# Two more weight slots in the rope tables' space around the first out-projection, and longer fillers in the four-step attention blocks

## The chip, the cores and the metric

One Trainium2 chip, 8 cores, one program on all of them. Each core computes 2 of the 16 sequences and exchanges nothing with the others. The metric is the device time of the slowest core in microseconds.

## The reference

One decoder layer on x of (16, 2048, 1024): a feed-forward half-step, a token mixer, a second feed-forward half-step, a last RMSNorm. Every sub-layer has an RMSNorm, a shift and scale on its input and a gate on its output, all three from `c @ w_ada`.

```python
u = modulate(rmsnorm(h, ffn1_norm), sh1, sc1)
h = h + 0.5 * g1 * ((silu(u @ w_gate) * (u @ w_up)) @ w_down)      # 1024 -> 2816 -> 1024
u = modulate(rmsnorm(h, mix_norm), sh2, sc2)
proj = u @ w_in                                                     # q, k, v and latents
# group A: 4 heads of differential attention, two softmax maps of width 64 each, rope on q and k
# group B: 4 heads of latent attention, width 64 + 32 (rope on the 32), causal as well
h = h + g2 * (concat([od, om]) @ w_out)
u = modulate(rmsnorm(h, ffn2_norm), sh3, sc3)
h = h + 0.5 * g3 * ((silu(u @ w_gate2) * (u @ w_up2)) @ w_down2)
return rmsnorm(h, final_norm)
```

## The kernel before, in words

**Tiles.** A core holds two sequences s = 0, 1 of 2048 positions, each as four tiles tt of 512 positions, with the 1024 channels as 8 pieces of 128 partitions. Intermediate h lives in DRAM. A tile is 2 MB in f32.

**Two lanes.** The program is written out in full by Python generators; each `yield` gives a cost. Lane F (`lane_f`, `ffn_group` L580) is the feed-forward work; lane M (`lane_m`, `mixer` L967) is the token mixer. The loop at the end of `build` takes one step of lane M, adds what it yields to `credit`, and then takes steps of lane F until their costs (0.216, named MM, for one matmul of 512 columns) have used the credit up. So each yield of lane M is the amount of filler, in these credit us, that is put behind that step on PE. Where lane M yields None it stands, and lane F goes on alone. When lane M is done, lane F runs alone. The order on each engine is the order in which the generators issue; engines then run by semaphores.

**Lane F.** First sequence 0, then sequence 1 while mixer(0) runs (tiles named 10 to 13 in the code), then the second feed-forward of sequence 0 (20 to 23) while mixer(1) runs, then, once mixer(1) is done, that of sequence 1 in two groups of two tiles. For one tile, `unit` L596 runs 11 times: two units of 2048 columns of weights (gate and up), 4 x 8 matmuls, tanh on ACT and two products on DVE. Then 8 down steps of 22 matmuls on two weight units of 1408 columns, with a residual piece that is loaded (`Residual`) and stored. In the two-tile groups the first tile's two first units come before the second tile's.

**Weights.** `Ring` L189 holds the slots: NWF = 6 for lane F (wf), 4 for the mixer (wm). `plan` lists all loads in order; `pump` issues the next one as soon as a slot is free; `release` frees a slot at the end of its use and pumps. A pair of wf slots is a unit or a down step, so with 6 slots the pairs of the next two are on their way. The loads of wf go through the SP queue, in order with all its other transfers; a transfer that waits for an engine holds up those behind it. The wm loads are casts on the POOL queue.

**The norms of lane F** are side generators (`norm_gen` L465): load a tile into XT, some steps of lag (8, or 14 where `dense`), 8 squares and 8 statistics matmuls, one step for the rsqrt on ACT, 8 applies. `f_step` advances them by one step for each step of lane F, or for every second one while both lanes run. With `dense` it is every one. A group that needs a tile waits in program order until its norm is written out.

**mixer(s).** At its start it loads the first two tiles (MIXP, and MUS with a row of 2 KB pieces) and the rope tables (`load_tab` L767, eight transfers of 128 KB into TAB). Norms of four tiles, each step yielding W_NORM. For a = 0, 1: projections of two heads with rope (it reads TAB), then `attention` L790 over two heads (g = 0, 1), each with four blocks qc = 0 to 3 of 4 qc + 4 steps. Then load_tab again with the latent layout, latents, and for a = 0, 1 up-projections (`rope` again) and `attention` with one group for two latent heads. Then the out-projection: for each tile 8 output pieces m, with a store of h and a load of the next tile's residual in halves, through the SP queue. TAB is idle from the last up-projection of mixer(0) to the start of mixer(1).

**attention.** Step i issues the scores of step i+1, exp on ACT, and the value matmuls of step i. At a block's end the sums are copied to `accsb` and `evac` puts the rest on `evq`: for a differential head ten small DVE parts ("D") and a transpose on PE ("T"). These run in the next block's steps; in a block of four steps all ten D parts are issued in its first step, and T at the earliest two steps later. At the start of each attention call `evq` is empty. A step yields at L864:

```python
yield W_ATT * (1.0 if r == 0 else 0.6)      # W_ATT = 1.2; r = 0 where the step has all four query blocks
```

In a block with qc = 0 the four steps have r = 0, 1, 2, 3. A step with a T yields 0.5 and 0.6 of W_ATT instead.

Of the kernel before, what the change touches and what calls it, by code (L numbers as in the profile page):

```python
# [157 lines left out]
NWF = 6  # L158
NWM = 4
MM = 0.216  # L160
W_ATT = 1.2
# [27 lines left out]
class Ring:  # L189


    def __init__(self, n):
        self.free = list(range(n))
        self.pending = collections.deque()
        self.loaded = {}
        self.on = False

    def plan(self, key, load):
        self.pending.append((key, load))
# [10 lines left out]
        return self.loaded[key]  # L210

    def release(self, key):
        self.free.append(self.loaded.pop(key))
        self.pump()

def build():
# [28 lines left out]
    sgu = [dscr(f"sgu{i}", [22, 128, 2048], BF16) for i in range(2)]  # L245
    sdn = [dscr(f"sdn{i}", [16, 128, 1408], BF16) for i in range(2)]

    with contextlib.ExitStack() as es:
# [4 lines left out]
        def sb(name, shape, dt):  # L253
            return es.enter_context(nc.sbuf_tensor(name, list(shape), dt))
# [24 lines left out]
        WFR = [Res(f"wf{i}") for i in range(NWF)]  # L279
        WM = [sb(f"wm{i}", [128, 2048], BF16) for i in range(NWM)]  # L280
        WMR = [Res(f"wm{i}") for i in range(NWM)]
        XT = sb("xt", [128, 4096], F32)
        xtR = [Res(f"xt{k}") for k in range(NK)]
        HST = [tile(f"hst{i}", [128, 512], F32) for i in range(3)]
# [65 lines left out]
        def dma_group(into, of, stream, parts):  # L350

            first = S.dma("sp", r=of, w=into, stream=stream, out=parts[0][0], in_=parts[0][1])
            rest = [S.dma("sp", stream=stream, out=o, in_=i) for o, i in parts[1:]]
            for o in rest:
                o.deps = list(first.deps)
                first.dval = o.dval
            for o in rest:
                o.dval = first.dval
# [37 lines left out]
        def wf_plan(fi, ps, first, units):  # L396
            for kind, j in units:
                n = 2048 if kind == "gu" else 1408
                if first:
                    wf.plan((fi, ps, kind, j), cast_load(WF, WFR, "wf", (wgu if kind == "gu" else wdn)[fi][j], n))  # L400
                else:
                    def load(b, kind=kind, j=j, n=n):
                        res = (sguR if kind == "gu" else sdnR)[fi][j]
                        assert res.w is not None
                        S.dma("sp", r=[res], w=[WFR[b]], stream=f"wf{b}", out=WF[b][:, 0:n], in_=(sgu if kind == "gu" else sdn)[fi][j])
                    wf.plan((fi, ps, kind, j), load)

        GU = [("gu", j) for j in range(22)]
# [358 lines left out]
        def load_tab(s, diff):  # L767
            if diff:
                parts = [(slice(32 * r, 32 * r + 32), si, 64 * (1 - si), 32) for r in range(4) for si in range(2)]
            else:  # L770
                parts = [(slice(64 + 16 * r, 80 + 16 * r), si, 32 + 64 * (1 - si), 16) for r in range(2) for si in range(2)]
            dma_group(tabR, tabDR[s], "tab", [(TAB[rows, si * 2048:(si + 1) * 2048].rearrange("p (t n) -> p t n", t=4),
                                               tabD[s, :, d0:d0 + n, :].rearrange("t p n -> p t n")) for rows, si, d0, n in parts])

        evq = collections.deque()
# [14 lines left out]
        def attention(groups, scale, evac, extra=()):  # L790
# [47 lines left out]
            for i in range(n):  # L838
                g, qc, j, r, last = steps[i]
                left = 4 * qc + 4 - j  # L840
                if evq and evq[0][0] == "T" and i >= tmin[0]:
                    tick(1)
                    pv(i)
                    yield 0.5 * W_ATT
                    if i + 1 < n:
                        qk(i + 1)
                    yield 0.6 * W_ATT
                else:
                    nd = 0
                    for kind, fn in evq:  # L850
                        if kind == "T":
                            break
                        nd += 1
                    if i + 1 < n:
                        qk(i + 1)
                    pv(i)
                    if not last:
                        for _ in range(-(-nd // max(1, left - 3))):
                            if evq and evq[0][0] == "D":
                                tick(1)  # L860
                                tmin[0] = i + 2
                    if extra and left > 2 and psF.free:
                        extra.popleft()()
                    yield W_ATT * (1.0 if r == 0 else 0.6)  # L864
            while extra:
                extra.popleft()()
            att[0] = False
# [99 lines left out]
        def mixer(s):  # L967
# [15 lines left out]
            def mstep(n):  # L983
# [7 lines left out]
                        mside.popleft()  # L991
                return False

            load_tab(s, True)
            for a in range(2):
                for tt in range(4):
# [105 lines left out]
            for a in range(2):  # L1102
# [34 lines left out]
                if a == 1:  # L1137
                    wm.release((s, "uq"))
                    wm.release((s, "ukv"))
                extra = []  # L1140
                if s == 0 and a == 0:
                    extra = [lambda: None] * 10 + [functools.partial(ada_unit, j, wm, WM, WMR) for j in range(32, 36)]
# [38 lines left out]
            for tt in range(4):  # L1181
                srcs = [gran(MIXB, mixR, h * 4 + tt) for h in range(4)] + [om_slot(h, tt) for h in range(4)]
                nxt = om_norm(tt + 1) if tt < 3 else iter(())
                for m in range(NK):
                    b = wm.get((s, "wo", m // 2))
                    wv = WM[b][:].rearrange("p (k n) -> p k n", k=8)
# [305 lines left out]
```

How the kernel before makes its waits and increments, by code:

```python
            def run(ename, eng):  # L109
                seen = {}
                for o in self.ops[ename]:
                    need = {}
                    for p in o.deps:
                        if p.dma:
                            key, val, sem = ("d", p.dsem), p.dval, dsem[p.dsem]
                        else:
                            key, val, sem = ("e", p.eng), p.tick, esem[p.eng]
                        if seen.get(key, 0) < val and need.get(key, (0, None))[0] < val:
                            need[key] = (val, sem)
                    waits = list(need.items())
                    fold = None
                    if FOLD_WAITS and waits and not o.dma:
                        fold = waits.pop()
                    for key, (val, sem) in waits:
                        eng.wait_ge(sem, val)
                        seen[key] = val
                    ins = getattr(eng, o.fn[0])(**o.fn[1])
                    if fold is not None:
                        key, (val, sem) = fold
                        ins._wait_ge(sem, val)
                        seen[key] = val
                    if o.dma:
                        ins.then_inc(dsem[o.dsem], 16)
                    elif o.inc:
                        ins.then_inc(esem[ename], 1)
                if ename == "sp":
                    for p in final_waits:
                        eng.wait_ge(dsem[p.dsem], p.dval)
```

## Time and profile before

| | us |
|---|---|
| median of 3 runs | 3069.78 |
| lowest, highest | 3059.08, 3070.62 |
| the profiled execution's own time | 3066.18 |
| its span, slowest core (core 1) | 3064.6 |
| the other cores' spans | 3034.3 to 3063.4 |
| PE busy | 2842.9 |
| DVE, ACT busy | 1403.2, 1254.9 |
| mean granted TensorE clock of core 1 | 0.980 |

The span goes from the first to the last instruction of the slowest core. All durations below come from this one execution. "PE" is the matmuls, "SPq" the instructions of the SP queue that issue transfers; x is a count. An idle time in brackets stands before the row's first instruction, with the operation that released it. Every operation is recorded at line 127, the helper that issues it, so groups are told apart by their tiles: `uf,wf` are gate/up matmuls, `actf,wf` down-projection, `mu,wm` and `mixb,wm` the mixer's, `pt,ones_sb` and `btf,ones_sb` the statistics of the mixer's and of lane F's norms, `cm_sb,obf` the transposes of evicted outputs.

### The profile page before, as it was taken

To read this page: it belongs to the slowest core of one execution; us is meant where nothing else is said; L and a number is where in the kernel's file an instruction comes from. 1 tells how busy PE (TensorE), PEld (TensorE's weight loads), DVE (VectorE), ACT (ScalarE), POOL (GpSimd) and SP (SyncE) were. 2 spreads that over 40 slices of the span, in tenths; PEclk is the share of its full clock that TensorE was granted. 3 is DMA by queue.
4 is the path that set the end of the run, shared out by engine and by line. 5 is a ranking of instruction groups with operands and counts; after the bars stand their busy time and mean duration, and the time that the engine had idled before them with its cause. 6 is when DMAs were issued, how large, how long until landed. Compare 5 with 4: busy or idle time off the path is not lost.

```text
span 3064.6 us, 42690 instructions; the slowest of 8 cores (3034.3 to 3064.6 us)
## 1 busy us (share of the span) xinstructions
PE 2842.9 (93%) x16528; PEld 1356.0 (44%) x16528; DVE 1403.2 (46%) x2808; ACT 1254.9 (41%) x1750; POOL 75.0 (2%) x147
## 2 busy tenths in 40 slices
PE   3799998999899999999978999999999999999998
PEld 1344443444454444544434445444454444444443
DVE  3564215344455455244446545654535443532532
ACT  2421205345434456444245443555755524322311
POOL 1000000000000000000000000000000000000000
PEclk9899999999999999999989999999999999999999
DMA  9886685475914934553883333434345278336436
GB/s 193 170 160 154 168 218 158 134 206 129 219 62 115 201 99 105 119 153 112 247 265 117 96 110 113 140 100 131 86 137 162 99 251 262 138 106 203 165 119 224
DMA packets 144138, 470.76 MB, mean 154 GB/s; under 512 B 17376, under 2 KB 21216, under 8 KB 129760
## 3 DMA queue, kind: packets, MB, share of 16 engines
q1 hardware_dynamic: 127600, 399.80, 40.9%
q0 software_dynamic: 16336, 68.23, 14.2%
q8 instruction: 131, 2.15, 0.3%
q14 instruction: 71, 0.58, 0.1%
HBM read 452.83 MB, written 100.66 MB: 181 GB/s over the span
## 4 chain that ended last, share of the span: by engine, by line
PE 76%; DMA 11%; ACT 5%; DVE 5%; issue 1%; SPq 1%; POOL 0%; ACTq 0%; DVEq 0%; POOLq 0%
PE psall L127 76%; ACT pt L127 3%; DMA wf<-sdn 2%; DMA wm<-w_ada 1%; DMA h<-hst 1%; DMA h<-qk 1%; DMA wf<-w_ada 1%; DMA accsb<-pos 1%; DMA hst<-xL 1%; SPq L127 1%; ACT mu L127 1%; DVE mu L127 1%; DVE ftm L127 1%; DVE accsb L127 1%; ACT L127 1%
## 5 line engine op out<-in xcount | busy, mean ns | idle before, releaser
L127 PE MATMUL psall<-uf,wf 128*128 128x512 bf16 x4224 | 1037.1, 384 | 30.5 <-DVE hst L127 6.6
L127 ACT ACTIVATE pt<-psall 128x1024 bf16<-128x1024 f32 (+3 forms) x520 | 453.0, 872 | 457.3 <-PE psall L127 455.8
L127 PEld LDWEIGHTS psall<-uf,wf 128*128 128x128 bf16 x4224 | 400.2, 99 | 462.5 <-issue 28.7
L127 PE MATMUL psall<-actf,wf 128*128 128x512 bf16 x2112 | 516.3, 386 | 16.8 <-DMA wf<-sdn 16.8
L127 ACT ACTIVATE ftf<-psall 128x512 f32<-128x512 f32 x352 | 210.1, 597 | 660.0 <-PE psall L127 645.9
L127 DVE SCALAR_TENSOR_TENSOR ftf<-ftf,psall 128x512 f32<-128x512 f32 x352 | 241.1, 685 | 448.0 <-ACT ftf L127 416.8
L127 PE MATMUL psall<-mu,wm 128*128 128x512 bf16 (+2 forms) x1312 | 328.6, 381 | 12.5 <-ACT mu L127 8.2
L127 PE MATMUL psall<-mixb,wf 128*128 128x512 bf16 x1408 | 321.4, 383 | 8.6 <-ACT mixb L127 4.9
L127 PEld LDWEIGHTS psall<-actf,wf 128*128 128x128 bf16 x2112 | 200.7, 99 | 227.6 <-issue 20.2
L127 DVE SCALAR_TENSOR_TENSOR hst<-psall,SC,hst 128x512 f32<-128x512 f32 x120 | 90.0, 750 | 426.1 <-PE psall L127 315.3
L127 DVE TENSOR_TENSOR actf<-ftf,psall 128x512 bf16<-128x512 f32 x264 | 180.9, 685 | 195.2 <-PE psall L127 192.7
L127 PE MATMUL psall<-va,pt 128*128 128x129 bf16 x3264 | 268.5, 222 | 1.7 <-ACT pt L127 1.6
L127 PE MATMUL psall<-qk 64*128 64x512 bf16 (+1 forms) x960 | 201.3, 354 | 44.6 <-ACT pt L127 36.9
L127 PEld LDWEIGHTS psall<-va,pt 128*128 128x128 bf16 x3264 | 202.0, 98 | 65.8 <-issue 39.8
L127 PEld LDWEIGHTS psall<-mixb,wf 128*128 128x128 bf16 x1408 | 137.3, 98 | 178.4 <-ACT mixb L127 8.1
L127 PEld LDWEIGHTS psall<-mu,wm 128*128 128x128 bf16 (+2 forms) x1312 | 130.2, 102 | 177.5 <-ACT mu L127 16.6
L127 DVE TENSOR_TENSOR ftm<-tab,psall 128x512 f32<-128x512 bf16 (+1 forms) x208 | 139.6, 683 | 114.6 <-PE psall L127 94.5
L127 ACT ACT_TABLE_LOAD x92 | 118.0, 1283 | 158.5 <-PE psall L127 156.4
L127 PEld LDWEIGHTS psall<-qk 64*128 64x128 bf16 (+1 forms) x960 | 55.5, 94 | 228.4 <-ACT pt L127 143.0
L127 ACT ACTIVATE btf<-xt 128x512 bf16<-128x512 f32 x164 | 97.9, 623 | 99.1 <-DMA xt<-xL 43.0
L127 ACT ACTIVATE btm<-psall 128x512 bf16<-128x512 f32 (+1 forms) x104 | 61.7, 594 | 136.1 <-PE psall L127 135.3
L127 DVE COPY accsb<-psall 128x387 f32<-128x387 f32 x144 | 74.0, 514 | 57.6 <-PE psall L127 55.3
(113 smaller groups left out, 1991.5 us busy)
## 6 DMA issues: line engine op xcount, KB each, us to landing
wf<-sgu SPq DMA_DIRECT2D x242, 512.0 KB, 3.9
wf<-sdn SPq DMA_DIRECT2D x192, 352.0 KB, 4.1
h<-hst SPq DMA_DIRECT2D x120, 256.0 KB, 4.5
xt<-h SPq DMA_DIRECT2D x30, 1024.0 KB, 7.1
wm<-w_ada POOLq DMA_DIRECT2D x32, 512.0 KB, 12.1
hst<-xL SPq DMA_DIRECT2D x64, 256.0 KB, 6.4
qk<-h SPq DMA_DIRECT2D x16, 1024.0 KB, 6.5
h<-qk SPq DMA_DIRECT2D x16, 1024.0 KB, 9.7
```

The source lines that it names most:

```text
L127: ins = getattr(eng, o.fn[0])(**o.fn[1])
```

## The change

`Ring` learns to lend: `lend` adds slots to the free ones, `ask_back` takes those out that are free and keeps the others from coming back, `returned` says whether none is still loaded. Two slots, number 6 and 7, are the two halves of TAB (512 KB each). They are lent in mixer(0) after the last up-projection, asked back at the start of its fourth out-projection tile, and each mixer waits (`yield None`) until they are returned before it loads its tables. Loads into them also wait for the readers of TAB, and table loads for the readers of the slots. The yield of an attention step with qc = 0 becomes 1.2 where it has no eviction part and 1.7 x 1.2 = 2.04 where it has.

```diff
--- before.py
+++ after.py
@@ -194,6 +194,21 @@
         self.pending = collections.deque()
         self.loaded = {}
         self.on = False
+        self.lent = []
+        self.back = True
+
+    def lend(self, slots):
+
+        self.lent, self.back = list(slots), False
+        self.free += self.lent
+        self.pump()
+
+    def ask_back(self):
+        self.back = True
+        self.free = [b for b in self.free if b not in self.lent]
+
+    def returned(self):
+        return not any(b in self.lent for b in self.loaded.values())
 
     def plan(self, key, load):
         self.pending.append((key, load))
@@ -210,7 +225,9 @@
         return self.loaded[key]
 
     def release(self, key):
-        self.free.append(self.loaded.pop(key))
+        b = self.loaded.pop(key)
+        if not (self.back and b in self.lent):
+            self.free.append(b)
         self.pump()
 
 def build():
@@ -279,6 +296,9 @@
         WFR = [Res(f"wf{i}") for i in range(NWF)]
         WM = [sb(f"wm{i}", [128, 2048], BF16) for i in range(NWM)]
         WMR = [Res(f"wm{i}") for i in range(NWM)]
+        WF += [TAB[:, 0:2048], TAB[:, 2048:4096]]
+        WFR += [Res("wf6"), Res("wf7")]
+        lentR = {NWF: tabR[0:4], NWF + 1: tabR[4:8]}
         XT = sb("xt", [128, 4096], F32)
         xtR = [Res(f"xt{k}") for k in range(NK)]
         HST = [tile(f"hst{i}", [128, 512], F32) for i in range(3)]
@@ -402,7 +422,7 @@
                     def load(b, kind=kind, j=j, n=n):
                         res = (sguR if kind == "gu" else sdnR)[fi][j]
                         assert res.w is not None
-                        S.dma("sp", r=[res], w=[WFR[b]], stream=f"wf{b}", out=WF[b][:, 0:n], in_=(sgu if kind == "gu" else sdn)[fi][j])
+                        S.dma("sp", r=[res], w=[WFR[b]] + lentR.get(b, []), stream=f"wf{b}", out=WF[b][:, 0:n], in_=(sgu if kind == "gu" else sdn)[fi][j])
                     wf.plan((fi, ps, kind, j), load)
 
         GU = [("gu", j) for j in range(22)]
@@ -769,7 +789,7 @@
                 parts = [(slice(32 * r, 32 * r + 32), si, 64 * (1 - si), 32) for r in range(4) for si in range(2)]
             else:
                 parts = [(slice(64 + 16 * r, 80 + 16 * r), si, 32 + 64 * (1 - si), 16) for r in range(2) for si in range(2)]
-            dma_group(tabR, tabDR[s], "tab", [(TAB[rows, si * 2048:(si + 1) * 2048].rearrange("p (t n) -> p t n", t=4),
+            dma_group(tabR + WFR[NWF:], tabDR[s], "tab", [(TAB[rows, si * 2048:(si + 1) * 2048].rearrange("p (t n) -> p t n", t=4),
                                                tabD[s, :, d0:d0 + n, :].rearrange("t p n -> p t n")) for rows, si, d0, n in parts])
 
         evq = collections.deque()
@@ -861,7 +881,7 @@
                                 tmin[0] = i + 2
                     if extra and left > 2 and psF.free:
                         extra.popleft()()
-                    yield W_ATT * (1.0 if r == 0 else 0.6)
+                    yield W_ATT * ((1.7 if nd else 1.0) if qc == 0 else 1.0 if r == 0 else 0.6)
             while extra:
                 extra.popleft()()
             att[0] = False
@@ -991,6 +1011,8 @@
                         mside.popleft()
                 return False
 
+            while not wf.returned():
+                yield None
             load_tab(s, True)
             for a in range(2):
                 for tt in range(4):
@@ -1137,6 +1159,8 @@
                 if a == 1:
                     wm.release((s, "uq"))
                     wm.release((s, "ukv"))
+                    if s == 0:
+                        wf.lend([NWF, NWF + 1])
                 extra = []
                 if s == 0 and a == 0:
                     extra = [lambda: None] * 10 + [functools.partial(ada_unit, j, wm, WM, WMR) for j in range(32, 36)]
@@ -1181,6 +1205,8 @@
             for tt in range(4):
                 srcs = [gran(MIXB, mixR, h * 4 + tt) for h in range(4)] + [om_slot(h, tt) for h in range(4)]
                 nxt = om_norm(tt + 1) if tt < 3 else iter(())
+                if s == 0 and tt == 3:
+                    wf.ask_back()
                 for m in range(NK):
                     b = wm.get((s, "wo", m // 2))
                     wv = WM[b][:].rearrange("p (k n) -> p k n", k=8)
```

## Rows read from the trace of the kernel before

**Rows 1.** The page, busy time, share of the span and instructions of each engine.

```profile
PE 2842.9 (93%) x16528; PEld 1356.0 (44%) x16528; DVE 1403.2 (46%) x2808; ACT 1254.9 (41%) x1750; POOL 75.0 (2%) x147
```

**Rows 2.** Windows of 40 us: length, busy us of each engine, PEclk, DMA share, GB/s.

```profile
1480.00:1520.00 40.00, 40.00 (x187) 18.09 (x185) 17.43 (x26) 8.36 (x13) 1.09 (x2) 1.00 0.74 218
1520.00:1560.00 40.00, 28.84 (x120) 12.06 (x118) 12.99 (x20) 11.39 (x19) 1.06 (x2) 0.87 1.01 285
1560.00:1600.00 40.00, 28.45 (x108) 11.32 (x109) 15.85 (x26) 15.31 (x24) 0.00 (x0) 0.83 0.80 263
```

**Rows 3.** Waits of PE, 1310 to 1525 us: total us, times, longest; first of four.

```profile
PE psall L127 <- ACT pt L127: 4.9, 10, 1.2
```

**Rows 4.** Timeline of the SP queue at the end of the first out-projection (start, us, what).

```profile
1519.16 9.95 SPq L127 DMA_DIRECT2D h<-qk  x2
1529.27 1.07 SPq L127 DMA_DIRECT2D wf<-sdn  x2
...
1531.83 0.85 SPq L127 DMA_DIRECT2D mixb<-h  x2
1532.72 5.80 SPq L127 DMA_DIRECT2D mu<-h  x2
1538.67 14.46 SPq L127 DMA_DIRECT2D tab<-tabD  x8
1553.28 1.82 SPq L127 DMA_DIRECT2D wf<-sdn  x4
```

**Rows 5.** Timeline of PE in the same stretch, with idle time and releaser in brackets.

```profile
1549.75 0.61 PE L127 MATMUL psall<-pt,ones_sb 128*128 128x512 bf16 x1 [7.44 <-ACT pt L127]
...
1567.18 1.89 PE L127 MATMUL psall<-actf,wf 128*128 128x512 bf16 x4 [9.46 <-DMA wf<-sdn]
...
1579.56 1.97 PE L127 MATMUL psall<-mu,wm 128*128 128x512 bf16 x7
```

**Rows 6.** DMA view of 1525 to 1570 us.

```profile
DMA packets 5030, 12.92 MB, mean 287 GB/s; under 512 B 484, under 2 KB 1508, under 8 KB 4516
```

**Rows 7.** Timeline of PE: the transposes in the four second-head blocks with qc = 0.

```profile
776.44 0.79 PE L127 MATMUL psall<-cm_sb,obf 128*128 128x128 bf16 x4 [2.29 <-DVE obf L127]
...
1023.39 0.79 PE L127 MATMUL psall<-cm_sb,obf 128*128 128x128 bf16 x4 [2.81 <-DVE obf L127]
...
1787.13 0.79 PE L127 MATMUL psall<-cm_sb,obf 128*128 128x128 bf16 x4 [2.81 <-DVE obf L127]
...
2023.53 0.73 PE L127 MATMUL psall<-cm_sb,obf 128*128 128x128 bf16 x4 [1.21 <-DVE obf L127]
```

**Rows 8.** Windows of 10 us around these four transposes.

```profile
770.00:780.00 10.00, 7.51 (x50) 3.62 (x48) 6.65 (x25) 3.40 (x5) 0.00 (x0) 0.84 1.17 145
...
1020.00:1030.00 10.00, 6.63 (x27) 2.36 (x25) 6.10 (x20) 1.96 (x4) 0.49 (x1) 0.66 0.79 99
...
1780.00:1790.00 10.00, 6.99 (x47) 3.23 (x45) 7.81 (x27) 2.65 (x4) 0.00 (x0) 0.86 0.13 37
...
2020.00:2030.00 10.00, 8.20 (x60) 3.65 (x57) 8.33 (x28) 4.59 (x7) 0.00 (x0) 1.00 0.27 90
```

**Rows 9.** Timeline of PE, a first-head block with qc = 0.

```profile
1699.86 0.34 PE L127 MATMUL psall<-qk 64*128 64x384 bf16 x2 [0.25 <-ACT pt L127]
```

**Rows 10.** Timeline of PE behind the second mixer.

```profile
2567.98 4.44 PE L127 MATMUL psall<-actf,wf 128*128 128x512 bf16 x12 [2.38 <-DMA wf<-sdn]
...
2579.38 0.38 PE L127 MATMUL psall<-btf,ones_sb 128*128 128x512 bf16 x1
...
2585.63 13.98 PE L127 MATMUL psall<-uf,wf 128*128 128x512 bf16 x64
2599.45 2.75 PE L127 MATMUL psall<-mixb,wf 128*128 128x512 bf16 x12
```

**Rows 11.** Timeline of ACT in the same stretch.

```profile
2589.91 0.81 ACT L127 ACTIVATE mixb<-xt,SC 128x512 bf16<-128x512 f32 x1
```

**Rows 12.** Window from 2600 us to the last group's end.

```profile
2600.00:3058.00 458.00, 453.90 (x2103) 205.48 (x2100) 170.82 (x251) 115.64 (x180) 0.00 (x0) 1.00 0.48 155
```


## The prediction

> **What bounds the kernel now.** I read the page's busy shares first. TensorE (PE) is busy 93% of the span, VectorE and ScalarE under half [rows 1]. The matmuls are not changed, so only two things can move the time: PE's idle time of about 220 us and stretches at a lower granted clock. So I then looked for the stretches where PE idles near the code that is edited, in the windows, the timeline and the DMA view.
>
> Around the first out-projection the windows say where nothing is lost: in 1480 to 1520 us PE is busy 40.00 of 40 us. The loss comes right behind it: 28.8 and 28.5 of 40 us, at a granted clock of 0.87 and 0.83 [rows 2]. There the SP queue issues, in one burst, the last store of the out-projection, two down-projection weights, two residual tiles, 2 MB for the next mixer's first tile, 2 MB for its second and 1 MB of rope tables. The eight table issues hold the queue for 14.46 us; only behind them come the next four weights, at 1553.28 [rows 4]. PE stops twice: 7.44 us for the first square of the mixer's norm (its tile lands late) and 9.46 us for a down-projection weight [rows 5]. In 45 us the engines moved 12.92 MB, 287 GB/s [rows 6]: this burst is bound by transfers.
>
> **Edit 1: the lent slots.** The feed-forward lane (F) runs 11 gate/up units of 32 matmuls and then 8 down steps of 22 for each tile; the mixer lane (M) hands it credit at each yield, 0.216 a matmul. Walking the code's yields: at the lend point F is in the last down step of tile 2, and the ring holds that step's pair and the pairs of units 0 and 1 of tile 3. The lent pair takes unit 2, then every fourth pair: units 6 and 10. From then on each pair is issued one unit earlier. In the time of the loan the four waits of PE that the view lists are for ScalarE and VectorE, the longest 4.9 us in ten pieces, and none is for a weight [rows 3]; so that alone is worth 0. ask_back comes in the fourth out-projection tile, with F in unit 10, after unit 9's release. So the weights of down steps 0, 1 and 2 are all issued before the burst; today step 2's come behind it. Unit 10's release returns the pair 2.7 credit us before the second mixer starts: the new wait yields nothing, the table load finds its readers done, and nothing queues behind it. Cost of that wait: 0. If the pair were late, M would stand and F would run ahead by the same amount, with the price of edit 2's end.
>
> **Edit 2: the fillers.** In the four-step blocks (qc = 0) a step yields 1.2 instead of 0.72 when it has no eviction, and 2.04 instead of 1.2 when it has. The first block of each of the four attention calls of a mixer gains 3 x 0.48 = 1.44, the same block of a second head 0.84 + 0.48 + 0.48 = 1.80. Two mixers: 2 x (4 x 1.44 + 2 x 1.80) = 18.7 us of F work that is done earlier, 9.36 of it before the first mixer ends.
>
> **What the fillers win.** In the second heads' blocks PE waits for the evicted output to be scaled before it transposes it: 2.29, 2.81, 2.81 and 1.21 us [rows 7]. Of the new filler 0.84 + 0.48 = 1.32 us lie ahead of that transpose: 3 x 1.32 + 1.21 = 5.2 us. The three longer waits stand in windows of 0.84, 0.66 and 0.86 granted clock, the 1.21 one in a window of 1.00 [rows 7, 8]. The missing 1.6 + 3.4 + 1.4 = 6.4 us of clock lie partly over idle time; I take half, 3 us. The other blocks wait some 0.25 us at one step [rows 9]: eight of them, 2 us. Bounds: 5 us (the waits by 1.32, no clock) and 15 (all of it). A loss is excluded: it is work moved, not added. Sum: -10.
>
> **The burst, moved against F.** Today step 2's weights (needed 16.2 credit us after the second mixer starts) are what PE waits for. In the new order the first weights behind the burst are step 3's, needed 889.3 - 877.7 = 11.6 after it. Measured from the last store's issue (1528.8, just before its row ends), today the weight lands at 1567.18, 38.4 us later [rows 4, 5]. The new burst lacks 0.7 MB of weights and 0.5 MB of residual tiles ahead of it; at 287 GB/s [rows 6] that is 4.2 us, so step 3's weights land at 34. PE gets to them after 11.4 + 8 statistics matmuls (0.216 each) = 13.1 us: one wait of 21, in which the norm's tile lands too, against 7.44 + 9.46 today. Behind it lie 13.1 + 1.7 us of work to the first projection and about 2 of slow clock: 51 after the store. Today the projection starts at 1579.56 [rows 5], 50.8 after it. F is 9.4 ahead of M both at the start and at the end of this stretch. So the term is 0: the wait is not removed, it is one step later and one piece. Bounds: 12 us won (the weights land at 22, were the table issues not held up) and 6 lost (they land as late as today, and the clock falls longer).
>
> A page of the Trainium skill speaks for more here. "DMA: Bandwidth & Descriptors", under Bandwidth, gives each core of a pair that streams about 358 GB/s. At that rate the same bytes would land at 34 x 287 / 358 = 27, an estimate, and the sum would be 7 us lower than mine. The trace disagrees over the burst, with its 287 GB/s and 1,508 packets below 2 KB.
>
> **Where the moved work is missed.** At the second mixer's end F is 18.7 further on: 30 instead of 49 credit us of its tile 3 are left. They hide the norms of the next group's two tiles, one side step to each F step; the first takes 29 steps, the second 34. Today the 49 hold some 61 steps, and the second norm is done in time: its statistics end at 2579.76, the first tile's 64 matmuls begin at 2585.63, and only behind them, at 2599.45, is the second tile used [rows 10]. In the new order 30 credit us hold 38 steps and the 64 matmuls 16: 54 for 63, nine short. The last nine (the rsqrt and the eight applies) are then issued with no matmul between. What shows is the chain from the last statistic to the last apply, 2579.76 to 2590.72 today, 11 us [rows 10, 11]. Its last calls also queue behind lane F's; eight applies of 0.81 [rows 11] and some 2 for the rsqrt are 8.5. Less the 1.7 of matmuls that follow the applies one by one, 7. With the clock behind it 8.5: today 12 matmuls behind an idle 2.38 us took 4.44 instead of 2.6 [rows 10]. That wait of 2.38 itself, for weights beside a tile load, I leave as it is. After 2600 PE is busy 453.9 of 458 us [rows 12] and nothing else can be lost or won. Bounds: +3 (the applies run ahead of PE) and +13 (the whole chain and the clock). Sum: +8.5.
>
> **Sum.** -10 + 0 + 8.5 = -1.5 us on the profiled execution's 3066.2. The median of the runs shown is 3.6 above that execution: 3069.8 - 1.5 = 3068.
>
> **Rivals.**
> *The wait behind the burst shrinks.* If the table issues take their 14.46 us [rows 4] only because transfers are queued up in front of them, less in front lets step 3's weights go out up to 12 us earlier. For it: the rate reaches only 287 GB/s while SP stands. Against: POOL's casts of the mixer's weights and 5 MB of tiles and tables are unchanged. The Trainium skill's rate above would give a part of it, 7 us. It gives 3068 - 12 = 3056, and with the fillers' upper bound 3051. Chance 0.22.
> *The fillers fill nothing.* The 1.32 us are spent in other steps than the one that waits, or PE's order makes the wait reappear at the exp of the next step. Then the end's 8.5 stand alone, less 2: 3076. Against: the wait is a chain of some 7 us on VectorE that starts before both filled steps. Chance 0.12.
> *Slower: the wait behind the burst grows.* Place: down step 3 of F's tile 3. The cover is 11.6 against 16.2 today. The new order loses from the point where the weights land more than 34 us after the last store; each us later is a us of PE. If the mixer's tile and the tables go first and the weights land at 46, it costs 12 + 2 of clock: 3082. For it: the same queue, weights last. Chance 0.11.
> *The change doesn't do what it says:* the loan carries three pairs, none of which is waited for today [rows 3]. That is my own case for edit 1; its only effect is where step 2's weights stand.
> My case, with all waits moved and none of them gone, has 0.55.
>
> **Range and chances.** Low: -15 - 12 + 3 = -24, 3046. High: -5 + 6 + 13 = +14, 3084. Half a per cent, 15 us, is about what a measurement of this kernel can tell from no change. The first rival crosses it about every second time, and some of my own case does where the end costs little: faster 0.22. Slower by 15 needs the third rival with its full price or two bad bounds together: 0.08. Same: 0.70.
>
> **What would show it.** Right: the waits of the four transposes fall to 1.0, 1.5, 1.5 and 0, with a clock of 1.00 there; no weight wait at step 2 but one of 18 to 24 us at step 3, beginning some 13 us after the last store; six weights of the down steps ahead of the tables in SP's list; at the end a wait of 5 to 10 us on ScalarE's applies into the second tile, before its first unit. Wrong: the two waits behind the burst together below 12 us, a wait of the second mixer for the slots, or an end without that stop (then I am 8 us high).

## The result, and the profile after

The changed kernel takes 3091.8 us (median, 3090.2 to 3096.2), the kernel before 3067.3 on the same chip: ratio 1.0086, 95% interval 1.0062 to 1.011. The medians differ by 24.5 us, and 3091.8 lies outside the predicted range of 3046 to 3084; "slower" had been given 0.08. The profiled execution took 3096.2 us; the mean span of its eight cores is 3077.5 us, against 3047.4 in the profiled execution of before. I use these means below, because single cores of one execution differ by 28 to 30 us. In some executions of every kernel the cores of one die get a lower clock; these are left out of all ratios and averages, and a kernel with too few others has no ratio.

The page of the changed kernel, span and busy times (its counterpart of [rows 1]):

```profile
span 3094.6 us, 42679 instructions; the slowest of 8 cores (3066.5 to 3094.6 us)
...
PE 2858.1 (92%) x16528; PEld 1358.9 (44%) x16528; DVE 1403.5 (45%) x2808; ACT 1264.2 (41%) x1758; POOL 74.9 (2%) x147
```

The work is the same, and PE is busy 15 us longer, so part of the loss is clock. In the mean of eight cores PE's waits grew from 203.0 to 217.6 us, and the time lost to the clock (the length of each stretch times what its granted clock lacks to 1.00) from 47.5 to 65.5; some of the second lies over idle time, so the two can't be added. The next step was to cut both traces at the same places of the program. The table gives the mean of eight cores, in us. Attention blocks are numbered 0 to 23 in each mixer (24 to 47 in the second); block n ends where the first copy of its sums to `accsb` begins. Since lane F moves against lane M, a stretch can hold more or fewer matmuls (the fourth column); the last column takes 0.216 us off for each one more.

| from the end of | before | after | matmuls | difference, corrected |
|---|---|---|---|---|
| start to block 0 | 687.8 | 691.5 | +10 | +1.5 |
| block 0 to 4 | 86.4 | 83.0 | -9 | -1.5 |
| **block 4 to 6** | 44.1 | 55.4 | +16 | **+7.8** |
| block 6 to 12 | 201.9 | 198.9 | +2 | -3.4 |
| **block 12 to 15** | 77.0 | 89.6 | +15 | **+9.4** |
| **block 15 to 16** | 114.1 | 123.3 | +8 | **+7.5** |
| block 16 to the last store of the first out-projection | 306.8 | 304.8 | +1 | -2.2 |
| that store to block 24 | 176.1 | 164.9 | -61 | +2.0 |
| block 24 to 36 | 320.8 | 324.0 | +20 | -1.1 |
| **block 36 to 40** | 192.7 | 202.3 | +14 | **+6.6** |
| block 40 to 44 | 121.7 | 121.8 | +1 | -0.1 |
| **block 44 to the second out-projection** | 109.2 | 116.4 | +6 | **+5.9** |
| the rest | 608.8 | 601.5 | -24 | -2.1 |

So the loss sits in five stretches, 37 us together, and the prediction names none of them. What it does name came out small. The rows below are those of core 7, the slowest.

PE's timeline at the transposes (to be held against [rows 7]), then a window around the first (against [rows 8]):

```profile
778.28 0.73 PE L127 MATMUL psall<-cm_sb,obf 128*128 128x128 bf16 x4 [1.00 <-DVE obf L127]
...
1032.66 0.73 PE L127 MATMUL psall<-cm_sb,obf 128*128 128x128 bf16 x4 [1.01 <-DVE obf L127]
...
1815.43 0.73 PE L127 MATMUL psall<-cm_sb,obf 128*128 128x128 bf16 x4 [1.44 <-DVE obf L127]
...
2056.05 0.73 PE L127 MATMUL psall<-cm_sb,obf 128*128 128x128 bf16 x4 [0.60 <-DVE obf L127]
```

```profile
774.00:784.00 10.00, 8.88 (x62) 4.09 (x61) 7.62 (x27) 5.22 (x8) 0.00 (x0) 1.00 1.12 154
```

The fillers fill: the waits of 2.29, 2.81, 2.81, 1.21 us have become 1.00, 1.01, 1.44, 0.60, with a granted clock of 1.00 in the window (0.84 in that of before).

The burst behind the first out-projection, SP queue and PE (against [rows 4, 5]), and its DMA rate in 1570 to 1615 us (against [rows 6]):

```profile
1553.67 13.89 SPq L127 DMA_DIRECT2D h<-qk  x2
...
1571.91 11.65 SPq L127 DMA_DIRECT2D tab<-tabD  x8
1583.71 1.51 SPq L127 DMA_DIRECT2D wf<-sdn  x2
```

```profile
1595.97 1.86 PE L127 MATMUL psall<-actf,wf 128*128 128x512 bf16 x4 [16.97 <-DMA wf<-sdn]
...
1614.72 1.24 PE L127 MATMUL psall<-mu,wm 128*128 128x512 bf16 x5
```

```profile
DMA packets 5430, 12.04 MB, mean 268 GB/s; under 512 B 517, under 2 KB 1541, under 8 KB 5099
```

One wait of 16.97 us for one weight takes the place of the two of before. It begins 11.8 us after the last store (issued at about 1567.2), and the first projection starts 47.5 us after that store.

Now the first of the five stretches. VectorE's (DVE's) waits over the whole span, before (core 1) and after (core 7); the columns are total us, times, longest:

```profile
DVE hst L127 <- DMA hst<-xL: 97.6, 18, 14.4
```

```profile
DVE hst L127 <- DMA hst<-xL: 143.2, 21, 23.3
```

These are lane F's residual adds, waiting for a residual piece to be loaded. DVE's, PE's, SP's and GpSimd's timelines of the changed kernel in block 4 to 6:

```profile
801.21 0.75 DVE L127 SCALAR_TENSOR_TENSOR hst<-psall,SC,hst 128x512 f32<-128x512 f32 x1 [11.30 <-DMA hst<-xL]
801.87 0.42 DVE L127 COPY mixb<-psall 128x512 bf16<-128x512 bf16 x1
...
817.91 0.75 DVE L127 SCALAR_TENSOR_TENSOR hst<-psall,SC,hst 128x512 f32<-128x512 f32 x1 [11.13 <-DMA hst<-xL]
```

```profile
802.35 0.29 PE L127 MATMUL psall<-qk 64*128 64x128 bf16 x2 [5.81 <-DVE mixb L127]
```

```profile
779.46 0.32 SPq L127 DMA_DIRECT2D h<-hst  x1
779.82 4.61 SPq L127 DMA_DIRECT2D hst<-xL  x1
...
800.75 0.33 SPq L127 DMA_DIRECT2D hst<-xL  x1
```

```profile
760.43 0.53 POOL L127 DMA_DIRECT2D wm<-w_ada  x1 [2.48 <-PE psall L127]
760.95 0.98 POOL L127 DMA_DIRECT2D sgu<-wgu  x2
786.65 0.49 POOL L127 DMA_DIRECT2D sgu<-wgu  x1 [24.72 <-DMA sgu<-wgu]
```

The residual load issued at 779.82 reaches the add 21.4 us later, at 801.21. DVE executes in order, so the copy of the transposed attention output (`mixb`) behind the add is late, and PE waits 5.81 us for it. The next load goes into a buffer whose store must land first: the store of 779.46 takes until 800.7, the load goes out at 800.75, and the add at 817.91 is late again. The GpSimd rows say what is in flight: behind the mixer's weights the queue lets go a row of the 38 casts that prepare the second feed-forward's weights (`sgu<-wgu`; `convert`, every 11th step of lane F), which had queued behind weight loads waiting for their slots.

Before, the residual load was no faster: issued at 781.94, it reached its add 25.7 us later. But there the copy of `mixb` stood ahead of the add, so only DVE waited (core 1):

```profile
796.06 0.42 DVE L127 COPY mixb<-psall 128x512 bf16<-128x512 bf16 x1 [4.43 <-PE psall L127]
...
807.68 0.75 DVE L127 SCALAR_TENSOR_TENSOR hst<-psall,SC,hst 128x512 f32<-128x512 f32 x1 [8.22 <-DMA hst<-xL]
```

Lane F's lead has put the late add in front of the copy; that is what turns a wait of DVE into one of PE.

In block 15 to 16 PE's waits come to only 5.5 us against 2.2, but the clock falls: 4.9 us are lost to it against 0.0 (mean of cores). PE's two longest waits, and windows at three places (core 7, after):

```profile
1130.43 3.51 PE L127 MATMUL psall<-mu,wm 128*96 128x512 bf16 x8 [1.30 <-DVE accsb L127]
...
1167.85 0.40 PE L127 MATMUL psall<-cm_sb,obf 128*128 128x128 bf16 x4 [2.05 <-DVE mu L127]
```

```profile
1125.00:1135.00 10.00, 7.87 (x42) 3.71 (x41) 3.65 (x10) 3.34 (x5) 0.00 (x0) 0.83 0.32 79
...
1165.00:1175.00 10.00, 7.95 (x33) 3.45 (x32) 4.67 (x8) 4.92 (x9) 0.00 (x0) 0.83 0.18 55
...
1210.00:1220.00 10.00, 8.49 (x32) 3.16 (x33) 7.25 (x11) 7.21 (x12) 0.00 (x0) 0.83 1.04 260
```

In block 36 to 40 the reload of the rope tables stands behind a 2 MB tile and DVE waits for it:

```profile
2137.64 3.82 SPq L127 DMA_DIRECT2D xt<-h  x2
2141.56 2.16 SPq L127 DMA_DIRECT2D tab<-tabD  x4
```

```profile
2149.17 1.29 DVE L127 TENSOR_TENSOR ftm<-tab,psall 32x512 f32<-32x512 bf16 x2 [9.95 <-DMA tab<-tabD]
```

Before, the table reload was issued at 2097.98 and the tile at 2112.09, behind it. In block 44 to the out-projection it is DVE again (PE waits 2.9 us for `actf` and 2.1 for `obf`, mean of cores; before, 0 and 0.8), with 3.6 us more lost to the clock.

### The profile page after: what moved, and what is told of

It reads as the page before. It is cut to its first block, busy times and chain, and to the rows that moved or that the text cites. A ratio compares the mean times of both kernels' runs of the same rounds, so it can differ in the third digit from the quotient of the medians.

```text
span 3094.6 us, 42679 instructions; the slowest of 8 cores (3066.5 to 3094.6 us)
## 1 busy us (share of the span) xinstructions
PE 2858.1 (92%) x16528; PEld 1358.9 (44%) x16528; DVE 1403.5 (45%) x2808; ACT 1264.2 (41%) x1758; POOL 74.9 (2%) x147
## 4 chain that ended last, share of the span: by engine, by line
PE 74%; DMA 11%; ACT 6%; DVE 5%; issue 1%; SPq 1%; POOL 0%; ACTq 0%; DVEq 0%; POOLq 0%
PE psall L127 74%; ACT pt L127 2%; DMA hst<-xL 2%; DMA h<-hst 2%; DMA accsb<-pos 2%; DMA wm<-w_ada 1%; DMA wf<-w_ada 1%; SPq L127 1%; ACT mu L127 1%; ACT L127 1%; DMA wf<-sdn 1%; DMA h<-qk 1%; DVE ftm L127 1%; DVE accsb L127 1%; DVE mu L127 1%
## 5 line engine op out<-in xcount | busy, mean ns | idle before, releaser
L127 PE MATMUL psall<-uf,wf 128*128 128x512 bf16 x4128 | 1017.8, 385 | 23.2 <-DVE hst L127 5.9
L127 PEld LDWEIGHTS psall<-uf,wf 128*128 128x128 bf16 x4128 | 391.7, 99 | 445.4 <-issue 33.2
L127 PE MATMUL psall<-qk 64*128 64x512 bf16 (+1 forms) x960 | 203.0, 357 | 52.8 <-ACT pt L127 34.5
L127 PEld LDWEIGHTS psall<-va,pt 128*128 128x128 bf16 x3264 | 203.0, 98 | 67.6 <-issue 40.0
```

The lines of the kernel that those rows point to most:

```text
L127: ins = getattr(eng, o.fn[0])(**o.fn[1])
```

## The experiments

All ratios are to the kernel before, run on the same chip. Expectations number the blocks as above. "Mean of cores" is that of the profiled execution, to which the stretches belong; where the mean over all counted executions is given, the text says so. For before that second mean is 3046.1, 3044.3 and 3046.0 us on three chips, for the changed kernel 3072.8.

**First: which half of the change?** Two kernels, each with one half of the change: `fill_only` is before with the new yield line; `slots_only` is the changed kernel with the old one.

```
-  yield W_ATT * (1.0 if r == 0 else 0.6)
+  yield W_ATT * ((1.7 if nd else 1.0) if qc == 0 else 1.0 if r == 0 else 0.6)
```

> The kernel before with the new yields of the four-step blocks alone, no lent slots. Every instruction but the feed-forward weight loads then stands where it does in the changed kernel, lane F 9.36 credit us ahead of the first mixer at its end. Theory A (the loss of about 25 us comes from lane F's changed place against the mixer, and the slots are worth nothing): ratio 1.006 to 1.011, the transposes' waits at about 1 us as in the changed kernel, residual adds on VectorE waiting for their load behind the second head's first block. Rival B (the lent slots and their extra waits cost): 0.997 to 1.000, since the fillers alone then win.

> The changed kernel with the yields of before. Up to the lend point it is the kernel before. The lent pair then holds the weights of down step 1 when it is asked back, so the second mixer stands for 15.6 credit us of lane F before it loads its tables, and the rest runs with lane F that much further on. Theory A: no loss before the first out-projection; the two weight and tile waits behind it change, the sum within 12 us of before (ratio 0.996 to 1.004). Rival B: 1.006 or more, most of it where the slots are lent.

The slots alone: 1.0039 [1.0018, 1.0059], mean of cores 3049.9, within what was expected. On core 1 PE waits only 6.44 us for a down weight behind the burst, but the lent pair holds step 1's weights when it is asked back, and the tables go out 22.8 us behind the last store, against 9.9 before. That this gives the gain back is argued and not shown: the stretch from the last store to block 24 is 175.4 us, against 176.1. The fillers alone have no ratio: 3089.4 and 3099.9 us, and in a repeat (`fill_rep`) 3091.2 and 3125.0, against medians of 3062.4 and 3061.4 before. The profile of `fill_only` (mean of cores 3069.9, +22.5) shows the same bad stretches: block 4 to 6 53.3 us, block 36 to 40 203.1. So nearly all of the cost comes with the fillers, not with the slots.

**Is it their work, or the lead they give lane F?** `net0` is before with the fillers, and takes the same amount back in the full steps of the next block (qc = 1), so that lane F stands where it did. `phase_only` does the reverse: blocks as before, but lane F gets the same lead in one piece ahead of each attention call. (Code cuts here and below are shortened; text behind # is a remark.)

```
+  want = W_ATT * ((1.7 if nd else 1.0) if qc == 0 else 1.0 if r == 0 else 0.6)
+  if qc == 0:
+      debt[0] += want - W_ATT * (1.0 if r == 0 else 0.6)
+  elif qc == 1 and r == 0:
+      pay = min(debt[0], 0.48)
+      debt[0] -= pay
+      want -= pay
+  yield want
```

```
+  yield 3.24        # ahead of each differential attention call
   yield from attention([[(c, slice(0, 64))
...
+  yield 1.44        # ahead of each latent one
   yield from attention([[(0, slice(0, 96))
```

> The kernel before with the new yields in the blocks of four steps, and the same amount taken back from the full steps of the next block (at most 0.48 each), so that lane F stands where it did from there on. Theory A: the fillers win what they win (the four transposes' waits fall by 1.3 each, with the clock behind them some 6 to 10 us), and nothing of the loss is there: ratio 0.997 to 0.998. Rival C (longer fillers themselves hold up exp and the evictions): 1.003 or more, with longer PE waits for exp in these blocks.

> The kernel before, with the yields of the four-step blocks as they were and one extra yield ahead of each attention call (3.24 ahead of the differential ones, 1.44 ahead of the latent ones). Lane F then stands at the end of each attention call where it stands in the changed kernel, but no filler is added to the blocks that wait. Theory A (the place of lane F costs, the fillers win): slower than the kernel before by 20 to 32 us, a little more than the changed kernel (ratio 1.007 to 1.011), with the transposes' waits as in before. Rival C (the longer fillers cost by themselves, the place doesn't): 0.998 to 1.002.

> The same kernel as fill_only, which has no interval yet. Its one profile has a mean of the eight cores of 3069.9 against 3047.4 before. Theory A: ratio 1.006 to 1.011; rival B (slots): 0.999 to 1.003.

`net0`: 1.0016 [0.9998, 1.0034]. Expected was 0.997 to 0.998, so that is missed. Its profiled execution has a mean of cores of 3042.3, 5.1 below before, but it is the fastest of six: over all of them the mean is 3046.4, against 3046.1 before. The timeline of PE in `net0`:

```profile
772.95 0.73 PE L127 MATMUL psall<-cm_sb,obf 128*128 128x128 bf16 x4 [1.00 <-DVE obf L127]
...
1020.75 0.73 PE L127 MATMUL psall<-cm_sb,obf 128*128 128x128 bf16 x4 [1.11 <-DVE obf L127]
```

The transposes' waits are as short as in the changed kernel, and its loss isn't there (block 4 to 6 45.6 us, 36 to 40 191.6). `phase_only`: 1.0099 [1.0072, 1.0127], as expected, mean of cores 3073.5: no filler in the waiting blocks, and the whole loss (block 4 to 6 52.0, 15 to 16 122.8, 36 to 40 201.6). Its DVE and PE timelines:

```profile
801.21 0.75 DVE L127 SCALAR_TENSOR_TENSOR hst<-psall,SC,hst 128x512 f32<-128x512 f32 x1 [11.62 <-DMA hst<-xL]
```

```profile
802.35 0.29 PE L127 MATMUL psall<-qk 64*128 64x128 bf16 x2 [5.41 <-DVE mixb L127]
```

This settles it for the change: the lead alone costs 1%, the fillers without the lead neither cost nor win anything that a measurement of the whole can tell.

**Parts of the loss.** `after_tab` moves the second table load of each mixer ahead of the second differential attention call; `net0_tab` does the same on `net0`. `after_cv` lets the casts begin at lane F's 150th step, every 10th, instead of every 11th from the first on.

```
-  load_tab(s, False)                 # behind both attention calls
...
+  if a == 1: load_tab(s, False)      # behind the last rope of call 2
```

```
-  if cvn[0] % 11 == 0:
+  if cvn[0] >= 150 and cvn[0] % 10 == 0:
```

> The changed kernel, with the second table load of each mixer issued before the second attention call instead of behind it (the tables' readers are done there). In the changed kernel that load is issued behind a 2 MB tile load in the second mixer and VectorE waits some 10 us for it. If that wait is on the path, the kernel gets 5 to 9 us shorter than the changed one (3083 to 3087), all of it between the second attention's end and the first latent attention's start in mixer 1; if not, it stays at 3092.

> The kernel before with fillers moved inside two blocks (as net0) and the second table load issued before the second attention call. In one profile net0's mean over the cores was 5 us below the kernel before; the earlier table load should be worth 0 to 3 here, as nobody waits for it in the kernel before. Theory A: ratio 0.996 to 0.999; if small extra waits of the new places cost as much as the fillers win: 0.999 to 1.002.

> The changed kernel, with the 38 casts of the second feed-forward's weights spread from the 150th to the last step of lane F instead of from the first. Up to the end of the second head's second block of the first attention call (about 830 us) nothing but lane F and the mixer's own loads then uses the DMA queues. If the late residual pieces there (VectorE waits 11 and 19 us for hst in two stretches, and PE 4.7 us for the transposes' copies behind them) are late because of these casts, both waits go and that stretch gets 6 to 10 us shorter; later stretches may lose some of it. If they stay, the lateness is the queue's own order (store, then load into the same buffer).

`after_tab`: 1.0091 [1.007, 1.0111], 3089.3 us: no gain that can be told from the changed kernel's 1.0086, less than expected. DVE's wait for the tables is gone, but block 36 to 40 only fell from 202.3 to 200.0: of its 6.6 us some 2 were the tables. `net0_tab`: 1.0018 [1.0001, 1.0035], no gain, where 0.996 to 0.999 was expected. `after_cv`: 1.0083 [1.0045, 1.0121], 3082.0 us; here the stretches say more than the time. The start to block 0 fell from 691.5 to 677.3, block 4 to 6 from 55.4 to 40.7 (more than the 6 to 10 us expected), but block 12 to 15 rose from 89.6 to 98.7: ten casts now come there between 988 and 1051 us. The stop follows the casts. The queues and SP's 256 KB transfers in 765 to 825 us, with their median from issue to landing, in the changed kernel (core 7) and then in `after_cv` (core 3):

```profile
q0 software_dynamic: 616, 5.47, 67.9%
q1 hardware_dynamic: 2161, 5.58, 31.6%
...
h<-hst SPq DMA_DIRECT2D x4, 256.0 KB, 20.1
hst<-xL SPq DMA_DIRECT2D x4, 256.0 KB, 16.9
```

```profile
q1 hardware_dynamic: 4328, 11.73, 59.0%
q0 software_dynamic: 66, 0.85, 8.3%
...
h<-hst SPq DMA_DIRECT2D x7, 256.0 KB, 4.8
hst<-xL SPq DMA_DIRECT2D x6, 256.0 KB, 5.0
```

**Last: the casts spread by hand**, so that few leave the GpSimd queue in the two stretches where lane F stores and loads its residual tiles (in before, eight become three at 750 us and nine become five at 990 us; none in lane F's first 44 steps). Theory C of the expectations is that the heap of casts makes the residual loads late. The same edit on before, on the changed kernel, on it with the early tables, and on `net0` with the early tables.

```
-  if cvn[0] % 11 == 0:
+  if cvn[0] in CVP:
+  CVP = (45, 50, 55, 60, 65, 120, 135, 150, 176, 182, 188, 194, 225, 243, 261, 279, 297,
+         *range(305, 342, 6), *range(352, 389, 6), *range(394, 413, 3))
```

> The kernel before with only the order of the 38 weight casts of the second feed-forward changed: none in lane F's first 44 steps, five at steps 45-65, three (was eight) in the stretch that opens at 745-755 us, four at 929, five (was nine) at 994, the rest after 1160. Theory C (what makes the loads of the residual late is the heap of casts that the in-order GpSimd queue lets go behind the mixer's weight loads): the DVE waits for hst<-xL in 400-450 us and in 775-830 us go (60 and 13 us of waits now), first attention block some 10 us earlier as when the casts began late in lane F, 4 more from blocks 4 to 6: ratio 0.994-0.998. Rival (the lateness has nothing to do with the casts, which only moved a phase): first block 10 us earlier as seen once already, but blocks 4 to 6 as before: 0.996-0.999. Told apart by blocks 4 to 6 (44.1 us now) and by SP's transfers there (25 us to landing now, 5 by Theory C).

> The changed kernel with the same new order of the casts. Theory C: blocks 4 to 6 of the first mixer 55.4 -> about 41 us, blocks 12 to 14 50.2 -> about 42, start 10 us less; the three clock dips behind the last rope tables (9 us) and the second mixer's tables (7) stay: 3091.8 - 32 = 3060, ratio 0.994-1.000 to the kernel before. Rival (lane F's place costs it by itself, whatever is in flight): only the start's 10 us: 1.004-1.007.

> The same and the second table load of each mixer issued before the second differential attention call. Both theories: 2-3 us below the kernel without the moved table load, as seen before (2.5 us): 0.993-0.999 by Theory C, 1.003-1.006 by the rival.

> The kernel before, longer fillers paid back in the next block (lane F's place unchanged, no lent slots), early table load, and the new order of the casts. If the gains add: net0 with the early table load stood at 1.0018 (profile -0 to +2 us), the casts take 13: 0.995-0.999. If Theory C holds and lane F's place no longer matters once the heap is gone, this one and after_sp_tab stand within 0.002 of one another; by the rival after_sp_tab stands 0.005-0.008 above it.

| kernel | ratio | mean of cores | block 4 to 6 | 12 to 15 | 15 to 16 | 36 to 40 |
|---|---|---|---|---|---|---|
| before | 1 | 3047.4 | 44.1 | 77.0 | 114.1 | 192.7 |
| before_sp | 0.9948 [0.9916, 0.9981] | 3031.7 | 39.1 | 77.3 | 114.1 | 192.7 |
| after | 1.0086 [1.0062, 1.011] | 3077.5 | 55.4 | 89.6 | 123.3 | 202.3 |
| after_sp | 1.0023 [1.0009, 1.0037] | 3049.4 | 40.7 | 92.7 | 122.2 | 201.9 |
| after_sp_tab | none | 3051.9 | 40.7 | 91.7 | 123.2 | 200.3 |
| net0_sp_tab | 0.9924 [0.9895, 0.9953] | 3031.2 | 39.9 | 76.9 | 116.0 | 191.4 |

`after_sp_tab` took 3070.5 in its one counted execution. The ratio of `before_sp` fits Theory C, but its interval doesn't exclude the rival's 0.996 to 0.999; the stretches decide. Block 4 to 6 goes to 39.1 and 40.7, as Theory C has it and the rival hasn't. But `after_sp`'s 1.0023 misses both expectations: Theory C wanted block 12 to 14 to fall from 50.2 to about 42 us, and it is 52.9. The rows of SP and DVE in `after_sp` there (core 5):

```profile
1002.48 1.18 SPq L127 DMA_DIRECT2D h<-hst  x1
1003.76 0.58 SPq L127 DMA_DIRECT2D hst<-xL  x1
...
1026.59 0.33 SPq L127 DMA_DIRECT2D hst<-xL  x1
```

```profile
1030.80 0.75 DVE L127 SCALAR_TENSOR_TENSOR hst<-psall,SC,hst 128x512 f32<-128x512 f32 x1 [16.76 <-DMA hst<-xL]
```

The first store lands only after 24 us, and the second load of the fence has to wait for that. The mixer's weights have landed before it goes out, the last at 997.2 us; what is in flight while the store takes its 24 us is two casts at a time.

And they aren't the five casts of the plan. The step numbers in `CVP` are lane F's, and its lead brings seven of them to this place (983 to 1030 us; as many in `after_sp_tab`), against five in `before_sp` and `net0_sp_tab`. So with the lead the spreading took only two of nine casts out of this place, and it doesn't test what they cost there.

Casts in flight are not the whole of it either. From the first weight load of that heap to lane F's first store it is 41.1 us before and 26.8 after. In both, two casts are in flight as the store lands, yet the load that needs this store's buffer goes out 10.1 us behind it before and 24.6 after; why was not taken apart (GpSimd and SP, before on core 1, then after on core 7):

```profile
996.78 0.56 POOL L127 DMA_DIRECT2D wm<-w_in  x1 [53.67 <-PE psall L127]
...
1037.87 2.20 SPq L127 DMA_DIRECT2D h<-hst  x1
...
1047.93 3.49 SPq L127 DMA_DIRECT2D hst<-xL  x1
```

```profile
1007.00 0.56 POOL L127 DMA_DIRECT2D wm<-w_in  x1 [47.04 <-PE psall L127]
...
1033.84 1.34 SPq L127 DMA_DIRECT2D h<-hst  x1
...
1058.45 0.33 SPq L127 DMA_DIRECT2D hst<-xL  x1
```

So the casts explain all of the loss in block 4 to 6, and some 9 us at the start that before loses too (14 in the changed kernel). Most of the loss stays. With the same `CVP` in both, the changed kernel is still 1.0023 / 0.9948 = 1.0075 of the kernel before; over all counted executions the means are 3053.3 and 3032.8, 20.5 us apart, where they were some 27 apart. In blocks 15 to 16 and 36 to 40 the spreading changed next to nothing, so there lane F's lead costs without this heap; in block 12 to 15 the casts are not excluded.

`after_sp_tab` and `net0_sp_tab` differ by 20.7 us in the means of one execution each, 0.7%, as the rival had it. `net0_sp_tab`, 0.9924 where 0.995 to 0.999 was expected, beats both kernels, with 3040.0 to 3049.4 us; against `before_sp` its mean over all executions is only 2.9 us lower (3029.9), so nearly all of the gain is the casts'.

## Why the prediction was wrong

**The lent slots: right.** The loan went as walked through (unit 2 first, back in unit 10, no wait), down steps 0 to 2 stand ahead of the tables in SP's list. Alone they are 1.0039; without the fillers' lead the pair comes back late. The prediction's 0 took the loan only together with the lead, so this doesn't test it.

**What the fillers win: the waits as predicted, the gain at most half.** In the profiled execution, corrected for matmuls, the four stretches with the filled blocks (0 to 4, 8 to 12, 24 to 28, 32 to 36) gave -1.5, -2.2, -2.9 and +1.3, together -5.3. Predicted was -10. The waits fell by 1.29, 1.80, 1.37 and 0.61, 5.1 in all, against the 5.2 of the prediction; the 5 us for clock and other blocks did not come. In the time of the whole no gain shows at all: `net0`, which has the fillers and no lead, is 1.0016 [0.9998, 1.0034]. Where its 5 us go stays open.

**"A loss is excluded: it is work moved, not added": this is the step that failed.** The sum has no term for what lane F's lead costs outside the burst and the end; it stood at 0 without a reason. `phase_only` shows that moving lane F by 3.24 and 1.44 us ahead of the attention calls costs 1% by itself (3076.6 against 3044.3 us, mean over all counted executions), and `net0` that the same fillers without the lead don't. I costed what the lead does at the two places where lanes F and M exchange buffers, the burst and the end, and took all the time around them as if only the count of matmuls mattered. But every transfer and every DVE instruction of lane F moves too, and in block 4 to 6 a late add came to stand ahead of a copy that PE wants. The profile of before held the warning: 97.6 us of DVE waits for `hst<-xL`, up to 14.4 us each. I had read PE's waits, where they show as next to nothing; at the add of 807.68 the copy that PE wanted had already run.

**The burst: 0 predicted, +2.0 measured.** One wait at step 3, beginning 11.8 us after the last store (13.1 predicted), 16.97 us long (21), projection at 47.5 (51). The term is near 0 as worked out, but one of its premises is wrong: lane F's lead is not the same on both sides. By the table's matmul column lane F is 43 matmuls ahead at the last store and 18 behind at block 24; the working also counts 11.4 where it had derived 11.6. The rate in the burst was 268 GB/s [rows 6 have 287]. The Trainium skill's page "DMA: Bandwidth & Descriptors", Bandwidth, gives about 358 GB/s for each core of a pair that streams; the trace disagrees here as before.

**Where the moved work is missed: +8.5 predicted, nothing measured.** There is no wait for the second tile's applies. From 2584.74 to 2650 us, the stretch behind the out-projection, PE is held up only by

```profile
2604.37 2.75 PE L127 MATMUL psall<-actf,wf 128*128 128x512 bf16 x12 [0.47 <-DMA wf<-sdn]
```

The lead that was to be missed isn't there. The table's last row has 24 matmuls fewer, 5.2 us, and not 18.7: the 61 fewer between the last store and block 24, 13.2 us, had taken the rest back. In that stretch lane M stands in places (it yields None) and lane F goes on alone. The prediction had added up yields and left that standing as long as before; why it became shorter was not taken apart.

**The rivals.** None came true. The slower one put a loss of 14 us at the burst; a loss of that kind (a late transfer behind a queue) came, but at other places and about twice as large. No rival had the lead itself as a cost.

## What to carry to other kernels

Where two instruction streams are interleaved by hand, a longer filler is also a shift of one stream against the other, for as long as nothing takes it back: pay it back soon, or cost what the shift does to every queue. Before that, list each engine's waits for transfers, not only those of the bound engine: a late load that hurts nobody today is a price for any shift. And background transfers issued from an in-order queue don't come out as spread as they were issued: behind a blocked load they leave in a heap. A schedule in step numbers of one stream moves with that stream: a kernel with another lead needs its own. And when one execution's profile shows a gain, average all executions before believing it.

## What the hardware showed

**With casts in flight, the SP queue's transfers land late.** In 765 to 825 us of the changed kernel the packets of the software queue (GpSimd's) were 616 and took 67.9% of 16 engines' 60 us, 1.06 us each; the SP queue's 2161 took 0.14 each (31.6%). There SP's 256 KB transfers landed after a median of 17 and 20 us (13 in before); without the heap, in `after_cv`, after 5. The Trainium skill's page "DMA: Bandwidth & Descriptors", Queues, rings and completion order, says that an engine takes a whole packet from one queue before it turns to the next. The two packet times fit that, but no run here shows the order of the packets itself.

**Short waits can cost clock, and the same wait need not.** In block 15 to 16 of the changed kernel three 10 us windows have a granted clock of 0.83, a mean of the levels 1.2 and 2.4 GHz that leaves 1.7 us of full clock lost in each. PE waited 0.83 and 1.30 us in the first, 2.05 in the second, 1.00 and 0.83 in the third. In before a wait of 1.19 and that same wait of 1.00 (for the mixer's rsqrt, `rsm`), each alone in its window, cost none:

```profile
1155.00:1165.00 10.00, 8.81 (x42) 4.04 (x40) 4.48 (x7) 7.67 (x11) 0.00 (x0) 1.00 0.28 100
...
1177.00:1187.00 10.00, 8.99 (x41) 3.62 (x40) 5.67 (x10) 9.36 (x14) 2.04 (x4) 1.00 0.85 172
```

Why lane F's lead makes for longer waits in that stretch, and what makes block 44 to the out-projection 6 us longer, I didn't take apart. `phase_only` shows that they come with the lead (122.8 and 115.6 us), not by which instruction.
